# The end of the first attention and the hand-over between projection and mixer in a three-part transformer kernel

## The reference

```python
# first model, attention: 16 heads in groups of 6, 5 and 5 (dilations 1, 4, 16)
s = where(mask, q @ k.T, NEG); m = max(s); e = exp(s - m); den = sum(e); o = (e / den) @ v
lse = m + log(den)
alpha = softmax(stack([logsumexp(lse_g) - log(n_g) for g in groups]))      # one weight per group and token
y = concat([o_g * 3 * alpha_g for g in groups]) @ w_out

# second model, token mixer (l = 0, 1)
p = h @ w_in                                       # u, va, q, k, v, iq, ik, iw
a_out = gelu(u) * (causal(w_s) @ gelu(va) + b_s)   # spatial gating, 512 columns
score = sum_h iw_h * relu(iq_h @ ik.T)             # the 128 best keys of each query are kept
b_out = softmax(q @ k.T over the kept keys) @ v    # 8 heads, 512 columns
y = concat([a_out, b_out]) @ w_out
```

## Time and profile before

| | |
|---|---|
| median of 3 runs | 3171.99 us (3170.36 to 3172.25) |
| time of the profiled execution | 3170.2 us |
| its span | 3168.5 us |
| granted TensorE clock, mean | 0.979 |
| TensorE busy | 3052.2 us (96%) |
| VectorE busy | 1755.7 us (55%) |
| ScalarE busy | 1194.9 us (38%) |
| GpSimd busy | 126.4 us (4%) |
| matmuls of L1778, one of the three passes, 512 columns each | 3920 (2800 + 1120) |

### The profile page before, as it was taken

How to read it: one execution, slowest core, us unless ns; L and a number is a source line. 1 busy time by engine, 2 the same in 40 slices (tenths; PEclk the granted TensorE clock), 3 DMA queues, 4 the chain that set the end, 5 groups by cost and what they waited for, 6 DMA issues and landing times.

```text
span 3168.5 us, 39431 instructions
## 1 busy us (share of the span) xinstructions
PE 3052.2 (96%) x14303; PEld 2515.0 (79%) x14303; DVE 1755.7 (55%) x2786; ACT 1194.9 (38%) x1707; POOL 126.4 (4%) x117
## 2 busy tenths in 40 slices
PE   7899999988999999999998999999999999999998
PEld 5788888876888878888777788887888877788887
DVE  6677624755776256652687666424332477743323
ACT  3423223464333244442335544324443243644422
POOL 0000000000000000000030000000000003000000
PEclk8999999998999999999999999999999999999999
DMA  3355333212564326633321356332333322023332
GB/s 113 113 183 187 120 99 95 87 41 74 169 197 151 99 80 199 198 97 100 91 82 58 100 181 201 98 98 82 99 93 99 101 77 87 28 87 95 97 106 73
DMA packets 262906, 351.31 MB, mean 111 GB/s; under 512 B 16664, under 2 KB 208536, under 8 KB 262808
## 3 DMA queue, kind: packets, MB, share of 16 engines
q1 hardware_dynamic: 240768, 270.57, 27.8%
q0 software_dynamic: 21360, 79.01, 7.7%
q10 hardware_dynamic: 680, 0.43, 0.1%
HBM read 348.75 MB, written 2.10 MB: 111 GB/s over the span
## 4 chain that ended last, share of the span: by engine, by line
PE 86%; DVE 8%; ACT 3%; issue 2%; DMA 0%; POOL 0%; SPq 0%; DVEq 0%; ACTq 0%
PE bank L1778 28%; PE bank L1780 27%; PE bank L1779 27%; DVE w_lo L1071 1%; ACT w_hi L643 1%; DVE sumsq L1084 1%; DVE a_score L1395 1%; ACT probs L943 0%; PE bank L2054 0%; DVE work L1124 0%; DVE h_lo L1130 0%; DVE rot L1352 0%; PE bank L2128 0%; DVE turned L1351 0%; PE bank L1819 0%
## 5 line engine op out<-in xcount | busy, mean ns | idle before, releaser
L1071 DVE TENSOR_TENSOR w_lo<-raw,w_hi 128x1024 fp32r<-128x1024 f32 x482 | 589.7, 1224 | 1209.8 <-ACT w_hi L643 1209.0
L1778 PE MATMUL bank<-h_hi,w_hi 128*128 128x512 f32 x2800 | 1103.7, 394 | 21.2 <-DVE h_lo L1130 11.6
L1780 PE MATMUL bank<-h_hi,w_lo 128*128 128x512 f32 x2800 | 1095.8, 391 | 0.0
L1779 PE MATMUL bank<-h_lo,w_hi 128*128 128x512 f32 x2800 | 1095.3, 391 | 0.0
L643 ACT ACTIVATE w_hi<-raw 128x1024 fp32r<-128x1024 f32 x508 | 538.1, 1059 | 1395.1 <-PE bank L1780 1390.6
L1778 PEld LDWEIGHTS bank<-h_hi,w_hi 128*128 128x128 f32 x2800 | 529.4, 189 | 136.7 <-issue 24.4
L1780 PEld LDWEIGHTS bank<-h_hi,w_lo 128*128 128x128 f32 x2800 | 528.9, 189 | 111.6
L1779 PEld LDWEIGHTS bank<-h_lo,w_hi 128*128 128x128 f32 x2800 | 529.8, 189 | 108.7
L1778 PE MATMUL bank<-act_hi,w_hi 128*128 (+1 forms) x1120 | 435.9, 389 | 1.0 <-DVE w_lo L1071 1.0
L1780 PE MATMUL bank<-act_hi,w_lo 128*128 (+1 forms) x1120 | 435.7, 389 | 0.0
L1779 PE MATMUL bank<-act_lo,w_hi 128*128 (+1 forms) x1120 | 435.7, 389 | 0.0
(11 more groups left out here) (293 smaller groups left out, 2424.8 us busy)
## 6 DMA issues: line engine op xcount, KB each, us to landing
raw<-in_ffn_w_in_dram SPq DMA_DIRECT2D x176, 512.0 KB, 3.5
ada_w<-in_ada_w_dram POOLq DMA_DIRECT2D x72, 1024.0 KB, 5.6
raw<-in_ffn_w_out_dram SPq DMA_DIRECT2D x88, 512.0 KB, 3.6
raw<-in_ffn_w_gate_dram SPq DMA_DIRECT2D x44, 512.0 KB, 3.9
raw<-in_ffn_w_up_dram SPq DMA_DIRECT2D x44, 512.0 KB, 3.9
raw<-in_ffn_w_down_dram SPq DMA_DIRECT2D x44, 512.0 KB, 3.8
raw<-in_mix_w_in_dram SPq DMA_DIRECT2D x44, 512.0 KB, 3.6
raw<-in_attn_w_qkv_dram SPq DMA_DIRECT2D x24, 512.0 KB, 3.7
```

The source lines that it names most:

```text
L1071: V.tensor_tensor(w_lo[:, nb % SPL, :], raw[:, nb % RAW, :], w_hi[:, nb % SPL, :].bitcast(F32), ALU.subtract).then_inc(s_lo, 1)
L1778: T.matmul(dst, wh, mh, start=first, stop=False)
L1779: T.matmul(dst, wh, ml, start=False, stop=False)
L1780: return T.matmul(dst, wl, mh, start=False, stop=last)
```

## The change

It touches two places.

In the first attention the head outputs from 6 on are read in steps and written in one run instead of the other way round. The turning of the sums is issued before the product of head 14, and the turning back before the product of head 15. The coefficient chain of VectorE has fewer links: the reciprocals and the weights 3/n (new columns of `small`) are prepared beside the exponential, and the three group sums are issued without waits between them. The selection matrix, the split of the coefficients and the 16 spreading matmuls go. In their place ScalarE repeats the coefficients of two heads over 64 columns each (`repeat_coefs`), and TensorE turns the result with four transposes (`spread_pair`), over four PSUM banks; 12 matmuls that compute nothing (`keep_warm`) stand before the first of them. The last four pairs are turned between the chunks of the first slab of `out0`.

In the mixers' projections slots 20, 21 and 22 hold 1, 5 and 2 rounds, and the mixer's units 0 to 7 one round each. The low part of slab 23 comes at the end of slot 22, behind the rounds; slab 24 is split in unit 0 (high) and unit 1 (low) of the mixer. The filling steps 0 and 1 are issued in the projection's end, ahead of the last pair of v tiles. `first_part` is otherwise unchanged (it moves out of `mix`), and `half_pair` calls `between(k)` behind the second column of chunk k.

```diff
-        OT0 = [0, 9, 13]
+        OT0 = [0, 8, 12]
+        SPREAD_BANKS = (6, 7, 4, 5)
...
-        LAST_ROUNDS = {20: 1, 21: 3, 22: 1}
-        MIX_ROUNDS = range(0, 22, 2)
+        LAST_ROUNDS = {20: 1, 21: 5, 22: 2}
+        MIX_ROUNDS = range(0, 8)
...
-        FILL, at = {}, 0
+        FILL, at = {}, 2
...
-                        split_hi(n + 2 + j)
+                        if not m or slot < 23:
+                            split_hi(n + 2 + j)
...
+                    if u == 0:
+                        split_hi(out + 1)
...
                     if h >= DILATED:
-                        dst, src = by_class(dst), classes(src)
+                        dst, src = dst.rearrange("p (j r) -> p j r", r=4), src.rearrange("p (r j) -> p j r", r=4)
                     nc.scalar.activation(dst, src, ACT.Copy).then_inc(s_o, 1)
+                def repeat_coefs(n):
+                    if n == 0:
+                        act.wait_ge(s_on, 1)
+                    if n >= 2:
+                        act.wait_ge(s_otr, n - 1)
+                    nc.scalar.activation(work[:, 2 + n % 2, :].rearrange("p (b h d) -> p b h d", h=2, d=HD),
+                                         a1["fine"][:, 5, :, 2 * n:2 * n + 2].unsqueeze(3).to_broadcast([P, NB, 2, HD]), ACT.Copy)\
+                        .then_inc(s_coefs0, 1)
...
+                o_out(nh - 2)
                 act.wait_ge(s_aw, 1)
                 nc.scalar.activation(a1["fine"][:, 1], a1["fine"][:, 0], ACT.Exp).then_inc(s_ae, 1)
-                act.wait_ge(s_otr, 1)
-                nc.scalar.activation(b_["cTh"][0:nh, :], bank[6][0:nh, :], ACT.Copy).then_inc(s_ch, 1)
-                for n in range(nh // 2):
-                    act.wait_ge(s_on, n + 2)
-                    nc.scalar.activation(a1["out_hi"][:, n, :], work[:, n % 2, :], ACT.Copy).then_inc(s_hhi, 1)
+                for n in range(nh // 2 + 2):
+                    if n < nh // 2:
+                        repeat_coefs(n)
+                    if n >= 2:
+                        c = n - 2
+                        act.wait_ge(s_on, c + 2)
+                        nc.scalar.activation(a1["out_hi"][:, c, :], work[:, c % 2, :], ACT.Copy).then_inc(s_hhi, 1)
...
-                        if not m or not POOL_LO[0] <= n + 2 + j - nb < POOL_LO[1]:
-                            if m and n + 2 + j == nb + POOL_LO[1]:
-                                dve.wait_ge(s_lo, n + 2 + j)
+                        if not m or n + 2 + j - nb < POOL_LO[0]:
...
+                        if m and slot == 22:
+                            dve.wait_ge(s_lo, nb + POOL_LO[1])
+                            split_lo(nb + POOL_LO[1])
...
+                    if u == 1:
+                        split_lo(out + 1)
...
-                    if s == n_steps - 4:
-                        dve.wait_ge(s_hlo, H0["attn0"])
-                        V.tensor_copy(sel[0:nh, 0:nh, :], ident[0:nh, 0:nh].unsqueeze(2).to_broadcast([nh, nh, HD])).then_inc(s_sel, 1)
                 F = bufs["fine"]
-                nmx, den = F[:, 6], F[:, 7]
+                share, coef, nmx, den = F[:, 2], F[:, 5], F[:, 6], F[:, 7]
+                least, ex, wsum, tot = F[:, 4, :, 1:2], F[:, 1], F[:, 3, :, 0:3], F[:, 4, :, 0:1]
+                third = 1.0 / len(HEAD_GROUPS)
+                here, there = slice(0, DILATED), slice(DILATED, 16)
+                def own(n):
+                    return bufs["sums"][:, 24 * n:24 * n + 24].rearrange("p (h b) -> p b h", b=NB)
+                def back(n):
+                    return bank[1][:, 0:20 * NB].rearrange("p (b h) -> p b h", h=20)[:, :, 10 * n:10 * n + 10]
                 dve.wait_ge(s_exp, n_steps)
-                for n, dst in enumerate((nmx, den)):
-                    V.tensor_copy(dst[:, :, 0:DILATED], bufs["sums"][:, 24 * n:24 * n + 24].rearrange("p (h b) -> p b h", b=NB))
+                V.tensor_copy(nmx[:, :, here], own(0))
+                link(V.tensor_scalar(den[:, :, here], own(1), third, None, ALU.mult))
+                V.reciprocal(coef[:, :, here], den[:, :, here])
                 dve.wait_ge(s_sumB, 1)
-                for n, dst in enumerate((nmx, den)):
-                    back = bank[1][:, 0:20 * NB].rearrange("p (b h) -> p b h", h=20)[:, :, 10 * n:10 * n + 10]
-                    ins = V.tensor_copy(dst[:, :, DILATED:16], back)
-                link(ins)
-                least, ex, wsum, tot = F[:, 2, :, 0:1], F[:, 1], F[:, 3, :, 0:3], F[:, 4, :, 0:1]
+                link(V.tensor_copy(nmx[:, :, there], back(0)))
                 link(V.tensor_reduce(least, nmx, AX_X, ALU.min))
                 V.tensor_tensor(F[:, 0], least.to_broadcast([P, NB, 16]), nmx, ALU.subtract).then_inc(s_aw, 1)
+                link(V.tensor_scalar(den[:, :, there], back(1), third, None, ALU.mult))
+                V.tensor_tensor(share, den, small[:, 67:83].unsqueeze(1).to_broadcast([P, NB, 16]), ALU.mult)
+                link(V.reciprocal(coef[:, :, there], den[:, :, there]))
                 dve.wait_ge(s_ae, 1)
-                link(V.tensor_tensor(ex, ex, den, ALU.mult))
+                link(V.tensor_tensor(ex, ex, share, ALU.mult))
                 for g, (lo, hi) in enumerate(HEAD_GROUPS):
-                    link(V.tensor_reduce(F[:, 3, :, g:g + 1], ex[:, :, lo:hi], AX_X, ALU.add))
-                    link(V.tensor_scalar(F[:, 3, :, g:g + 1], F[:, 3, :, g:g + 1], 1.0 / (hi - lo), None, ALU.mult))
+                    last = V.tensor_reduce(F[:, 3, :, g:g + 1], ex[:, :, lo:hi], AX_X, ALU.add)
+                link(last)
                 link(V.tensor_reduce(tot, wsum, AX_X, ALU.add))
                 link(V.reciprocal(tot, tot))
-                link(V.tensor_scalar(tot, tot, float(len(HEAD_GROUPS)), None, ALU.mult))
                 link(V.tensor_tensor(wsum, wsum, tot.to_broadcast([P, NB, 3]), ALU.mult))
-                link(V.reciprocal(F[:, 5], den))
                 for g, (lo, hi) in enumerate(HEAD_GROUPS):
-                    last = V.tensor_tensor(F[:, 5, :, lo:hi], F[:, 5, :, lo:hi],
+                    last = V.tensor_tensor(coef[:, :, lo:hi], coef[:, :, lo:hi],
                                            F[:, 3, :, g:g + 1].to_broadcast([P, NB, hi - lo]), ALU.mult)
                 last.then_inc(s_on, 1)
-                dve.wait_ge(s_ch, 1)
-                V.tensor_tensor(bufs["cTl"][0:nh, :], bank[6][0:nh, :], bufs["cTh"][0:nh, :].bitcast(F32), ALU.subtract).then_inc(s_cl, 1)
-                dve.wait_ge(s_o, nh)
                 for n in range(nh // 2 + 1):
                     if n < nh // 2:
-                        dve.wait_ge(s_otr, n + 2)
+                        dve.wait_ge(s_otr, n + 1)
+                        dve.wait_ge(s_o, 2 * n + 2)
                         if n >= 2:
                             dve.wait_ge(s_hlo, base + n - 1)
-                        V.tensor_tensor(work[:, n % 2, :], bufs["oT"][:, n, :], bank[7 - n % 2][:], ALU.mult).then_inc(s_on, 1)
+                        V.tensor_tensor(work[:, n % 2, :], bufs["oT"][:, n, :], bank[SPREAD_BANKS[n % 4]][:], ALU.mult)\
+                            .then_inc(s_on, 1)
...
-                    T.matmul(bank[4][:, 0:2 * P], ones_r[:], turn_hi[:].rearrange("p n c -> p (n c)"), start=True, stop=True)
+                    T.matmul(bank[dst][:, 0:2 * P], ones_r[:], turn_hi[:].rearrange("p n c -> p (n c)"), start=True, stop=True)
...
                     scores(m, 0)
+                    first_part(m, 0)
+                    first_part(m, 1)
...
+                    if s == n_steps - 1:
+                        for r in range(4):
+                            ins = T.transpose(bank[7][0:20, r::4], bufs["sums"][:, 48 + r::4], ident)
+                        ins.then_inc(s_sumT, 1)
                     if s % 2 and s + 3 < n_steps:
                     if s - 1 in DONE_AT:
                         values(DONE_AT[s - 1])
-                for r in range(4):
-                    ins = T.transpose(bank[7][0:20, r::4], bufs["sums"][:, 48 + r::4], ident)
-                ins.then_inc(s_sumT, 1)
-                values(nh - 1)
                 pe.wait_ge(s_sumA, 1)
                 for b in range(NB):
                     ins = T.transpose(bank[1][:, 20 * b:20 * b + 20], bufs["sumsT"][0:20, b * P:(b + 1) * P], ident[0:20, 0:20])
                 ins.then_inc(s_sumB, 1)
-                pe.wait_ge(s_on, 1)
+                values(nh - 1)
+                keep_warm(12, 0)
+                for n in range(4):
+                    spread_pair(n)
+            def spread_pair(n):
+                pe.wait_ge(s_coefs0, n + 1)
+                if n < 4:
+                    pe.wait_ge(s_o, (13, 13, 15, 16)[n])
+                else:
+                    pe.wait_ge(s_on, n - 4 + 2)
                 for b in range(NB):
-                    ins = T.transpose(bank[6][0:nh, b * P:(b + 1) * P], bufs["fine"][:, 5, b, 0:nh], ident)
+                    ins = T.transpose(bank[SPREAD_BANKS[n % 4]][:, b * P:(b + 1) * P], work[:, 2 + n % 2, b * P:(b + 1) * P], ident)
```

(11 more changed lines are left out.)

75 lines of the change are left out of this document (37 added, 38 removed).

## The result

The changed kernel takes 3136.31 us (median; 3135.64 to 3137.03), the kernel before beside it 3171.18: a ratio of 0.9893, 95% interval 0.9881 to 0.9905. The forecast was 3146, with a range down to 3138. The gain is 34.9 us instead of 25.0. The profiled execution has a span of 3134.7 us instead of 3168.5 and a mean granted clock of 0.986 instead of 0.979.

What follows compares the result with a forecast made beforehand. TensorE's back-to-back matmuls (86% of the chain) were taken as the bound, with gains only where it waits or is clocked lower. 9.2 + 0 + 15.8 = 25.0 us off 3170.2 gave 3145.2, put at 3146; range 3138 to 3157.

Steps and rivals of the forecast that it cites:

- (a): Attention's end: the sums come back ahead of head 15's product, so VectorE starts earlier; gain 1.2 us.
- (e): First slab of `out0`: the four other pairs are turned inside it; loss 1.4 us.
- (b): Attention's end: VectorE's shortened coefficient chain takes 3.1 us for its thirteen instructions against 4.27; gain 1.2 us.
- (c): Attention's end: last coefficient to first finished chunk takes 3.9 us instead of 5.9; gain 2.0 us.
- (d): Attention's end: TensorE spreads four pairs, not eight, and begins `out0` with the first chunk; gain 6.2 us.
- (f): Mixers' projections, slots 21 and 22: VectorE's added rounds, 4.1 us, fit the gap ahead of slab 23's low part; cost 0.
- (g): Each mixer's start: TensorE reaches unit 1 earlier; gain 7.0 us, 4.9 from the closed gap and 2 from the clock.
- (h): Each mixer, units 0 to 7: VectorE's eight rounds slow TensorE, 15.5 us for 13.4; 2.1 us paid back.
- (i): Each mixer, units 8 to 21: seven rounds fewer leave TensorE as the floor; gain 3.0 us (1.9 to 4.1).
- Rival 2: Mixers: VectorE becomes their bound, each mixer gives 4.5 us; 3152 us; chance 0.17.
- rival 1: First attention: ScalarE's head output copies fall to 0.59 us, 3.9 us less; 3142 us; chance 0.28.
- Rival 3: Attention's end gives only 5 us: small instructions still 0.27, clock low for the first slab; 3150 us; chance 0.08.

Runs made afterwards that it cites:

- e1: The changed kernel with the head outputs from 6 on written in steps again instead of read in steps; 3145.51 us, ratio 0.9917.
- e4: The changed kernel with all eight pairs of coefficients turned ahead of `out0`, none between the chunks of its first slab; 3138.63 us, ratio 0.9901.
- e12: The kernel before, unchanged, run once more for a second profile; 3168.97 us.
- e13: The kernel before with 20 empty matmuls ahead of the first attention's last two v tiles; 3169.51 us, ratio 0.9998.
- e14: The kernel of e13 with the head outputs from 6 on read in steps instead of written in steps; 3165.95 us, ratio 0.9984.
- e3: The changed kernel without the 12 empty matmuls ahead of the first turned pair of coefficients; 3136.05 us, ratio 0.9893.
- e6: The changed kernel with the rounds as before: 1, 3, 1 in slots 20 to 22, one in each of units 0, 2, ..., 20; 3139.76 us.
- e7: The changed kernel with the mixers' eight rounds in every other unit (0, 2, ..., 14) instead of units 0 to 7; 3137.05 us, ratio 0.9897.

## Why the prediction was wrong

The mixers' steps were right and the attention's steps nearly so; the miss is one term taken at 0, and the clock. The measured column is from the first trace of each kernel, (a) and the head outputs from e1, (e) and the clock at `out0` from e4, whose first slab has no turnings and runs at the full clock.

| step | forecast | measured |
|---|---|---|
| (a) sums back earlier | 1.2 | 1.3 |
| (b) coefficient chain | 1.2 | 1.6, less 0.2 ahead of it |
| (c) to the first chunk | 2.0 | 2.4 |
| (d) `out0` with the first chunk | 6.2 | 5.9 |
| (e) four turnings in the slab | -1.4 | -1.8 |
| clock at `out0` | 0 | +1.2 (+2.9 with e12) |
| head outputs | 0 | 3.9 |
| (f) and (g) gap gone, each mixer | 7.0 | 7.0 |
| (h) units 1 to 7 | -2.1 | -2.5 |
| (i) units 8 to 21 | 3.0 | 3.0 |
| outside the edits | 0 | 4.4 (1.7 with e12) |

**The head outputs are the step that failed.** The prediction priced a stepped read of PSUM by a stepped read of SBUF and took 0. The copies fell to 0.59 us, and the gain was 3.9 us from e1's sums to the changed kernel's and 3.6 in the medians of e13 and e14. That it equals the forecast's working for this case (8 x 0.49 = 3.9) is partly luck: a copy gives the pace only 0.42 (e1), eight of them 3.3, and the rest came at the attention's end, where the clock also stayed up. How the last 1.0 us divides between the copy and the clock isn't shown. The nearest row was near in shape and not in kind: what it shared with the old write was SBUF. The Trainium skill ("SBUF — State Buffer", section "Specifications (TRN2)") says that SBUF's lines hold 16 bytes and want at least two hits each; a step of four fp32 elements hits each line once. This trace agrees that such a step costs, on both sides: write 1.08, read 1.11, without steps 0.59 and 0.63; no run here tries another step. What the Trainium skill ("PSUM — Partial Sum Buffer", section "Specifications (TRN2)") says of PSUM's lines, which the prediction weighed, it says of matmuls, and it didn't hold for ScalarE's reads: 0.59 us with steps of 512 bytes.

**The clock at `out0`** stayed up. The prediction had +1.3 as one end of its range, and 1.2 came. But e3 shows that the 12 empty matmuls were worth only 0.5 of it: without them the clock falls earlier and is back when `out0` begins. The 0.7 us of loss at the other end came neither in the changed kernel nor in e3. And today's cost, which the prediction read as 1.3, isn't fixed: it is 1.2 in the first trace of the kernel before and 2.9 in e12.

**(b) and (c)** were a little too dear: the thirteen instructions ahead of the last three take 2.63 us, 0.20 each, the low end of the prediction's 0.20 to 0.27, where it took 3.1. **(e)** was too cheap by 0.4: a turning takes 0.44 us of TensorE's path, not 0.35.

**(h)**: VectorE is busy for 15.93 of 15.93 us; that is the forecast's 15.5 and its reason. e6 and e7 show that rounds in eight consecutive units cause the payback. Rival 2's price for it (4.4) didn't come.

**Outside the edits** the prediction assumed that nothing moves. 4.4 us moved in the first pair of traces. It takes both to leave the range, whose edge lies 1.7 us above the time: with rival 1's 3.9 alone the sum would have been 28.9 us and the forecast 3142, with the 4.4 alone also 3142, both inside. With rival 1 and the clock at `out0` it is 3141. The last 4 to 5 us could not be worked out from the trace of before; its own repetition differs by up to 2.5 us in a stretch. What could have been done is a wider range, since the falls lasted differently in almost every trace here.

**Sums that don't come out.** Beside its sum the prediction puts the same gain a second way (`out0` at 733.4 instead of 744.32, less 1.2 and 1.4). That is 8.3 us and not 9.2. By its terms `out0` begins at 733.7, and the 1.2 isn't to be taken off, since head 15's product lies in TensorE's wait. The sum by terms stands. Rival 3's 2.7 us for 24 matmuls at half the clock is too little: at 0.43 us each instead of 0.23 it is 4.8, some 3.5 more than before. Neither changes the forecast.

## What to carry to other kernels

Price an access pattern by a row of the same memory and the same direction, and if none exists give the saving a real chance instead of zero. Where two engines share the pace, a saving on one is only kept if the other has room: look at who is busy at the lower clock. Issue work ahead of its turn only where something keeps TensorE busy behind it, and spread VectorE's rounds over every other unit instead of packing them into consecutive ones (0.9 us of each mixer; the wait in slot 19 held two more for 0.2). Before a difference of a few microseconds is given to an edit, take a second trace of each kernel: here the second moved 1.5 us into the attention's share.
